# A decoder trunk on one core: half of the low weight parts in the feed-forward blocks come from a negated copy and an adding transfer

## The reference

```
x += 0.5 * (silu(rms(x) @ Wg) * (rms(x) @ Wu)) @ Wd        # FFN 1, width 2816
x += W_out [ gated chunk mixing ; RG-LRU recurrence ](rms(x) @ W_in)
x += 0.5 * (silu(rms(x) @ Wg') * (rms(x) @ Wu')) @ Wd'     # FFN 2, width 2816
x += sigmoid(rms(x) @ W_pg) * (p @ W_pp)
```

## Time and profile before

| | |
|---|---|
| median of 3 runs | 1993.19 us (1992.12 to 1994.08) |
| span of the profiled execution | 1992.3 us |
| the runs' median less this span | 0.9 us |
| PE busy | 1963.2 us, 99% |
| DVE, ACT, POOL busy | 51%, 34%, 7% |
| DMA, mean of the span | 96 GB/s |

### The profile page before, as it was taken

One profiled execution on the slowest core, in us unless ns is written; L12 is line 12 of the kernel. 1 busy time (PEld: TensorE's weight loads), 2 busy tenths in 40 slices (PEclk: granted clock), 3 DMA queues, 4 the chain that ended last, 5 costly groups with the idle time before them and its releaser, 6 DMA issues.

```text
span 1992.3 us, 38215 instructions
## 1 busy us (share of the span) xinstructions
PE 1963.2 (99%) x16072; PEld 1943.0 (98%) x16072; DVE 1010.2 (51%) x1216; ACT 674.7 (34%) x851; POOL 137.8 (7%) x181
## 2 busy tenths in 40 slices
PE   7999999999999999999999999999999999999997
PEld 6999999998999999999999999999999999999996
DVE  5444434568554344346754344346775543443465
ACT  5322322445433222124433122224544331221353
POOL 1000000130110000001100000002201000000012
PEclk9999999999999999999999999999999999999998
DMA  5222222322332222223322222222222222222241
GB/s 194 90 92 93 86 94 90 109 86 69 102 118 95 95 85 95 95 84 127 100 93 84 95 95 95 85 93 97 75 96 95 86 95 90 90 95 87 93 139 46
DMA packets 54131, 190.46 MB, mean 96 GB/s; under 512 B 6096, under 2 KB 8432, under 8 KB 54048
## 3 DMA queue, kind: packets, MB, share of 16 engines
q1 hardware_dynamic: 52576, 184.87, 27.3%
q0 software_dynamic: 1472, 4.38, 0.7%
HBM read 186.91 MB, written 2.31 MB: 95 GB/s over the span
## 4 chain that ended last, share of the span: by engine, by line
PE 97%; DVE 1%; DMA 1%; ACT 0%; issue 0%; SPq 0%; POOL 0%; DVEq 0%; ACTq 0%
PE main L433 92%; PE aux L559 2%; PE aux L507 1%; DMA raw<-weights_dram 1%; PE aux L433 1%; PE main L559 1%; PE aux L579 0%; PE aux L458 0%; PE main L632 0%; DVE x L1163 0%; DVE rstd_b L870 0%; DVE rstd_b L1158 0%; PE aux L582 0%; DVE rs L298 0%; SPq L308 0%
## 5 line engine op out<-in xcount | busy, mean ns | idle before, releaser
L433 PE MATMUL main<-part_hi,w_hi 128*128 128x260 f32 x5104 | 1031.8, 283 | 13.2 <-DVE part_lo L864 10.0
L433 PE MATMUL main<-part_hi,w_lo 128*128 128x260 f32 x5104 | 1029.3, 283 | 0.0
L433 PE MATMUL main<-part_lo,w_hi 128*128 128x260 f32 x5104 | 1027.1, 283 | 0.0
L433 PEld LDWEIGHTS main<-part_hi,w_hi 128*128 128x128 f32 x5104 | 788.2, 189 | 16.6 <-DVE w_lo L858 9.8
L433 PEld LDWEIGHTS main<-part_hi,w_lo 128*128 128x128 f32 x5104 | 786.8, 189 | 0.0
L433 PEld LDWEIGHTS main<-part_lo,w_hi 128*128 128x128 f32 x5104 | 784.9, 188 | 0.0
L858 DVE TENSOR_TENSOR w_lo<-raw,w_hi 128x1024 fp32r<-128x1024 f32 (+1 forms) x344 | 433.1, 1260 | 208.1 <-ACT w_hi L655 196.1
L655 ACT ACTIVATE w_hi<-raw 128x1024 fp32r<-128x1024 f32 (+1 forms) x344 | 355.9, 1038 | 245.5 <-PE main L433 239.1
L698 ACT ACTIVATE part_hi<-tmp 128x520 f32 x88 | 56.2, 639 | 437.4 <-DVE tmp L932 437.4
L693 ACT ACTIVATE tmp<-tmp 128x520 f32<-128x520 f32 x111 | 71.2, 641 | 354.8 <-DVE tmp L924 321.6
L941 DVE SCALAR_TENSOR_TENSOR x<-main,x 128x520 f32<-128x520 f32 x96 | 66.8, 696 | 225.5 <-PE main L433 225.4
(11 more groups left out here) (167 smaller groups left out, 655.2 us busy)
## 6 DMA issues: line engine op xcount, KB each, us to landing
raw<-weights_dram SPq DMA_DIRECT2D x344, 512.0 KB, 3.2
x<-x_in_dram SPq DMA_DIRECT2D x4, 520.0 KB, 7.7
y_out<-x SPq DMA_DIRECT2D x8, 260.0 KB, 2.7
mix<-p_in_dram POOLq DMA_DIRECT2D x2, 520.0 KB, 3.6
ln<-ln_dram POOLq DMA_DIRECT2D x2, 512.0 KB, 5.9
ws<-ws_dram POOLq DMA_DIRECT2D x2, 512.0 KB, 8.6
bs<-bs_dram POOLq DMA_DIRECT2D x2, 256.0 KB, 6.3
bd<-bd_dram POOLq DMA_DIRECT2D x8, 64.0 KB, 8.9
```

The costliest lines, as they stand in the source:

```text
L433: last = pe.matmul(ps[:, q, 0:HALF], ww[:, s, w], xx[:, k, q * HALF:(q + 1) * HALF], start=(a == 0 and b == 0), stop=(a == kts - 1 and b = ...
```

## The change

Of four units in a row in the gate and up part of an FFN, two lose their subtraction on DVE: the units u + 3 that are prepared behind a gate unit u. There are 88 of them (22 in each of the four blocks, listed in `DMA_LO`; the last one of each chunk is the second unit of its down projection). ACT, behind rounding `w_hi`, writes the negated rounded weights into `w_lo` (`scale=-1.0`) and counts `nhi`; POOL then issues a transfer of the same unit from HBM into `w_lo` that adds to what is there, so that `raw - w_hi` results; PE waits for that transfer's semaphore. The semaphore `wlo` becomes one for each slot, and SP's fetch of unit n now waits until PE is done with unit n - 4 (`unit`). PE's loops are partly written out, since its waits now differ from unit to unit.

```diff
+DMA_LO = []
+for _l in range(DEPTH):
+    for _u in (U_F1, U_F2):
+        _n = _l * UNITS + _u
+        for _t in FFN_CHUNKS:
+            DMA_LO += [_n + AHEAD + 2 * _k for _k in range(_t)]
+            _n += 2 * _t + XT
...
                 for s in range(SLOTS):
-                    sp.wait_ge(wlo, i * SLOTS + (s - SLOTS + 1))
+                    sp.wait_ge(unit, i * SLOTS + (s - SLOTS + 1))
                     sp.dma_start(raw[:, s, :].rearrange("p (a n) -> p a n", a=1),
...
+            def negated_lo(l, which):
+
+                for k in range(HT0):
+                    d = (2 * l + which) * HT0 + k
+                    pool.wait_ge(nhi, d + 1)
+                    pool.dma_start(w_lo[:, DMA_LO[d] % SLOTS, :], weights[DMA_LO[d], :, :],
+                                   accum_op=ALU.add).then_inc(wlo_dma[DMA_LO[d] % SLOTS], 16)
+
             load_layer(0)
             for l in range(DEPTH):
+                negated_lo(l, 0)
                 sums(4 * l + 1)
                 conv_states(l)
...
                 sums(4 * l + 2)
+                negated_lo(l, 1)
                 if l + 1 < DEPTH:
                     load_layer(l + 1)
...
             def weights_in(n):
-                pe.wait_ge(wlo, n + 1)
+                if n in DMA_LO:
+                    pe.wait_ge(wlo_dma[n % SLOTS], landed(n))
+                else:
+                    pe.wait_ge(wlo[n % SLOTS], cut(n))
...
                             function(i * 4 + (G + 2 * j), ACT.Silu, T(0), T(1))
-                            hi(i * 4 + (n + 2 * j + AHEAD), (2 * j + AHEAD) % 4, False)
+                            s = (2 * j + AHEAD) % 4
+                            hi(i * 4 + (n + 2 * j + AHEAD), s, False)
+                            act.activation(w_lo[:, s, :], raw[:, s, :], ACT.Copy, scale=-1.0).then_inc(nhi, 1)
                             split_hi(l, i * 2 + (h + j + 1), i * 2 + j)
...
                             dve.wait_ge(evac, i * 4 + (G + 2 * j + 1))
-                            lo(i * 4 + (n + 2 * j + AHEAD), (2 * j + AHEAD) % 4)
```

More of the change, by code:

```diff
@@ L77, with landed, cut @@
 HT = 2 * HT0 + XT
+DMA_LO = []
[5 more added lines that the diff above has]
+            _n += 2 * _t + XT
+def landed(n):
+    return 16 * sum(u <= n and u % SLOTS == n % SLOTS for u in DMA_LO)
+def cut(n):
+    return sum(u not in DMA_LO and u % SLOTS == n % SLOTS for u in range(n + 1))
 Y_ORDER = (MT, MT + 1, 0, MT + 2, 1, MT + 3, 2, 3)
@@ L198, in trunk @@
         whi = sem("whi")
-        wlo = sem("wlo")
+        wlo = [sem(f"wlo{s}") for s in range(SLOTS)]
+        wlo_dma = [sem(f"wlo_dma{s}") for s in range(SLOTS)]
+        nhi = sem("nhi")
         unit = sem("unit")
@@ L439, in weights_in, with weights_in_loop @@
             def weights_in(n):
-                pe.wait_ge(wlo, n + 1)
+                if n in DMA_LO:
+                    pe.wait_ge(wlo_dma[n % SLOTS], landed(n))
+                else:
+                    pe.wait_ge(wlo[n % SLOTS], cut(n))
+            def weights_in_loop(n, i):
+                s = n % SLOTS
+                if s % 2:
+                    pe.wait_ge(wlo_dma[s], i * 16 + (landed(n + SLOTS) - 16))
+                else:
+                    pe.wait_ge(wlo[s], i + (cut(n + SLOTS) - 1))
             def free_main(G, behind_v=0, layer=0):
@@ L466, in ffn, with up @@
                 for c, tiles in enumerate(FFN_CHUNKS):
-                    def up(n, G, par, first=False):
+                    def up(n, G, par, first=False, i=None, n0=None):
                         for j in range(2 * 2):
-                            weights_in(n + j)
+                            if i is None:
+                                weights_in(n + j)
+                            else:
+                                weights_in_loop(n0 + j, i)
                             free_main(G + j)
@@ L478, in ffn @@
                     par = main_slot(G)
[L479 to L484, removed]
+                    up(n, G, par, c == 0)
+                    with pe.Fori(1, tiles // 2) as i:
+                        up(i * 4 + n, i * 4 + G, par, i=i, n0=n)
                     n, G, h = n + 2 * tiles, G + 2 * tiles, h + tiles
-                    with pe.Fori(0, 2) as i:
+                    for i in range(2):
                         for j in range(4):
@@ L490, in ffn @@
                             kw = None
-                            if j == 0:
+                            if i + j == 0:
                                 kw = lambda a: pe.wait_ge(hlo, h - tiles + a + 1)
@@ L857, in lo @@
                 c = used(n)
-                dve.tensor_tensor(w_lo[:, s, 0:c], raw[:, s, 0:c], w_hi[:, s, 0:c], ALU.subtract).then_inc(wlo, 1)
+                dve.tensor_tensor(w_lo[:, s, 0:c], raw[:, s, 0:c], w_hi[:, s, 0:c], ALU.subtract).then_inc(wlo[s], 1)
             def x_lo(stat, o):
```

## The result

The changed kernel takes 2006.96 us in the median of 4 runs (2005.34 to 2008.03), beside 1993.63 us for the kernel before in as many runs (1992.12 to 1994.09): 1.0068 times as long, 95% interval 1.0055 to 1.0080. That is 13.3 us more, where 7.3 us were forecast. The kernel before was run again beside the experiments, in groups of 15, 27 and 17 runs with medians of 1992.74, 1992.49 and 1992.94 us; beside these the change is 14.0 to 14.5 us longer. The profiled execution has a span of 2005.1 us, 12.8 above that of before.

The account below looks back on a forecast made before the run. PE, busy 1963.2 of 1992.3 us, was taken as the bound. Stalls at four block starts, 1.9 + 5.4 = 7.3 us, gave a 1999.6 us span; with 0.9 us from span to median, 2000.5 us, range 1992.5 to 2055.

Parts of the forecast that it names:

- What bounds the kernel: Whole program: PE, busy 1963.2 of 1992.3 us; no FFN unit waits for `w_lo` from 30 us on.
- the removed work: FFN blocks: 88 subtractions, 111 us of DVE's time, worth nothing because DVE is not waited for there.
- Rival 3: FFN matmuls: PE itself gets faster, 4.8 us over 88 units, 1988.4 us with a hidden transfer; chance 0.04.
- The windows: Time a transfer may take before PE waits: 3.3, 3.9, 3.9, 3.9 us at the four FFN block starts.
- L: Adding transfer's time from issue to landing: 5.2 us, or 5.7 at the last three block starts.
- The sum: Four block starts: PE stalls of (5.2 - 3.3) + 3 x (5.7 - 3.9) = 7.3 us.
- each stall goes into the time: Behind the four block starts PE is without slack, so the 7.3 us of stalls lengthen the time.
- Rival 2: Steady part: transfer outlasts its window from L = 8.1 us; 62 us more at L = 8.9; chance 0.20.
- the steady window: Between block starts: a transfer may take 8.1 us from issue to landing before PE waits.
- What else moves, at nothing: SP's later fetch, the moved parameter load, POOL's order, added traffic and PE's written-out loops: no cost or gain.
- moved `load_layer(1)`: End of the second block's up part: one sum 2 us late, made good before the norm at 949 us.

Follow-up runs that it names:

- eight-fill kernel: The change with POOL filling a small unused tile eight times ahead of each adding transfer, issuing it about 4.5 us later: 2195.70 us, ratio 1.1015.
- filler: The change with sixteen matmuls into an unused buffer ahead of the wait of each block's fourth unit: 2003.81 us, ratio 1.0056.
- two-fill: The change with POOL filling a small unused tile two times ahead of each adding transfer, issuing it about 1.1 us later: 2016.64 us, ratio 1.0121.

## Why the prediction was right, and where it was short

**What bounds the kernel, and the removed work: right.** 88 subtractions off DVE are worth nothing: ratio 0.9998 for the kernel that keeps all of them off DVE and has no stall. Rival 3 (PE gets faster) has no support.

**The windows and L: right, with some luck in the tenths.** Estimated windows of 3.3 and 3.9 us, L of 5.2 and 5.7 and their difference of 7.3 us stand against four waits of 2.17, 1.81, 1.88 and 1.76 us, 7.6 in all, at 36, 578, 1025 and 1567 us, and none in the steady part. The 0.5 us that L got for sharing with SP's fetch don't show: issue to PE's restart is 5.3 to 5.5 us at all four starts. What the sum left out is the 0.3 us between the end of the negation and POOL's issue. At the last three starts the two nearly cancel. Later and sooner issue, and a shorter landing, moved the waits the way the windows say.

**The sum: short by a factor of 1.8.** The step that failed is its last sentence, "each stall goes into the time". It does, but a stall of PE isn't only itself. Behind three of four the granted clock fell to 0.5 and took 1.5 us each, and each restart took 0.25 more: 5.5 us that the sum hadn't. Filling the stalls with work (3.2 us back with 7.7 us more work, clock up in all four runs) and shortening them (waits down by 2.3 us, clock up) show that it hangs on the idling. What decides which stall is followed by the lower clock stays open. Rival 2's 62 us would have been short for the same reason: in the eight-fill kernel a 2.06 us stall cost 3.84. Two slips in the working change nothing of the forecast: the steady window is 8.0 us by its own numbers and not 8.1, and rival 2 at L = 10 us adds up to 115 us (25 + 13.6 + 76), not 105.

**"What else moves, at nothing".** Right for SP's later fetch (ratio 1.0003; only with the parameters moved back is it waited for, 1.1 us at one place), for ACT, POOL and the traffic (at most 3.2 us for 84 transfers). For the moved `load_layer(1)` it was mis-sized: 1.65 us in the profile. I looked at who waits for the parameters (made good) and not at what their transfers collide with. It is no fixed price. The same stretch takes 52.8 and 52.1 us in the filler and two-fill profiles, but 50.6 to 50.7, as before, in those of the first unit on VectorE and of both kernels with a sooner negation, which load the parameters at the same place in POOL's queue. Moving them back gave nothing. No comparison of medians singles the 1.65 us out.

**The profiled time against the runs.** I took 0.9 us between the span and the median. In the results a run's time is 1.8 us above the span of the same run (2006.93 and 2005.1). So is it for before: the profiled execution, with its span of 1992.3 us, took 1994.08, one of the longer of its kernel. The forecast time of 2000.5 us should so have been about 1 us higher for a like execution, or 1999.8 to 2000.2 from the larger groups' medians; the forecast difference of 7.3 us isn't touched.

By medians then: 7.6 us of stalls, 4.6 of clock, 1.0 of restarts and 1.65 of crowding are 14.8, where 13.3 were measured beside four runs of before, and 14.0 to 14.5 beside the larger groups. This holds for the profiled execution, near the median of its kernel. Which starts lose clock differs between executions: in the profile with the parameters ahead it was the third that escaped. The mean clock of the change's four runs is 0.995, 0.994, 0.994 and 0.997, the last in the shortest, 2005.34 us; that one is only 1.6 us below the median, less than the clock would suggest, and the cause of that is open.

## What to carry to other kernels

A stall of a PE that is otherwise always busy can cost nearly twice its length (3.84 us for 2.06, and 1.5 times on average over 59 stalls): read the granted clock behind each new stall, and add what it shows. When work moves to a longer path, the average window says little; work out the window at the starts of the blocks, where a norm or another late factor holds the chain back, and put the first step of the long path ahead of what waits there. One line's place in ACT's order was worth 14 us here, and taking 107 us off an engine that nobody waited for was worth nothing.

## What the runs showed of the hardware

- Granted clock 0.50 to 0.51 for about 3.3 us behind stalls of 2.17, 1.81 and 1.88 us of PE, 1.00 behind one of 1.76, behind four of 1.2 to 1.4, and in other kernels behind ones of 2.07, 2.99 and 3.45 us, with 0.52 behind one of 1.89. Length alone doesn't decide.
- An adding transfer of 512 KB from HBM into the matmul's format: 5.4 us from issue to landing in the median and 0.87 us of POOL, the plain one 3.5 and 0.53 us.
- A 512 KB fetch issued among nine parameter transfers (16 to 512 KB) landed after 9.45 us, where 3.3 is the median.
